# Differential attention with its units in a mixed order, and gates applied as tiles become complete

## The reference

```python
def diff_attn_core(q, k, v, lam):
    s = jnp.einsum('bqhmd,bkhmd->bhmqk', q, k).astype(F32) * (B_HEAD_DIM ** -0.5)
    p = jax.nn.softmax(s, axis=-1)
    a = p[:, :, 0] - lam * p[:, :, 1]
    return jnp.einsum('bhqk,bkhd->bqhd', a.astype(v.dtype), v)

def b_post(o, z, length):
    o = rms_norm(o, subln_w, SUBLN_EPS) * (1.0 - lam_init)
    return o.reshape(bsz, length, B_WIDTH) * jax.nn.silu(z)
```

## Time and profile before

| | |
|---|---|
| median of 3 runs | 1922.96 us (1922.60 to 1924.41) |
| the profiled execution | 1921.78 us, its span 1920.1 us |
| PE busy | 1633.2 us (85%) |
| weight loads of PE | 1167.0 us (61%) |
| DVE busy | 931.6 us (49%) |
| ACT busy | 535.8 us (28%) |
| POOL busy | 150.6 us (8%) |
| DMA | 353.07 MB, mean 184 GB/s |

### The profile page before, as it was taken

One profiled execution on the slowest core, in us unless ns is written; L12 is line 12 of the kernel. 1 busy time (PEld: TensorE's weight loads), 2 busy tenths in 40 slices (PEclk: granted clock), 3 DMA queues, 4 the chain that ended last, 5 costly groups with the idle time before them and its releaser, 6 DMA issues.

```text
span 1920.1 us, 22864 instructions
## 1 busy us (share of the span) xinstructions
PE 1633.2 (85%) x8468; PEld 1167.0 (61%) x8468; DVE 931.6 (49%) x1602; ACT 535.8 (28%) x881; POOL 150.6 (8%) x226
## 2 busy tenths in 40 slices
PE   6799999797969799989499997777699989898980
PEld 6688888586858678777388896466534333333330
DVE  3875634765556556655757674665311111111114
ACT  3313122674132254542422563113111101010111
POOL 1000010132001000000101000110000000000002
PEclk9899999598979899989799997788699999999995
DMA  8224352003223120324134012035399999999993
GB/s 348 88 88 166 114 187 88 12 17 116 99 77 132 66 77 1 131 92 162 65 143 161 1 45 88 1 107 245 128 409 422 422 423 422 423 423 423 422 385 137
DMA packets 55795, 353.07 MB, mean 184 GB/s; under 512 B 7408, under 2 KB 7664, under 8 KB 18720
## 3 DMA queue, kind: packets, MB, share of 16 engines
q1 hardware_dynamic: 43056, 306.88, 39.9%
q0 software_dynamic: 12656, 45.07, 6.3%
HBM read 332.26 MB, written 23.59 MB: 185 GB/s over the span
## 4 chain that ended last, share of the span: by engine, by line
PE 60%; DMA 16%; DVE 15%; ACT 3%; SPq 2%; issue 2%; POOL 1%; DVEq 0%; POOLq 0%; ACTq 0%
PE ps L1834 11%; PE ps L1835 10%; PE ps L1836 10%; DMA early<-in_experts 9%; PE ps L2237 6%; PE ps L2020 5%; PE ps L1884 4%; DMA raw<-in_experts 3%; PE ps L2258 3%; SPq L604 2%; PE ps L2218 2%; PE ps L2042 2%; PE ps L1813 2%; ACT p L847 1%; DMA early<-in_ada 1%
## 5 line engine op out<-in xcount | busy, mean ns | idle before, releaser
L1834 PE MATMUL ps<-whi,xth 128*128 128x512 f32 (+1 forms) x768 | 301.6, 393 | 13.0 <-DVE tmp L1168 4.6
L1835 PE MATMUL ps<-wlo,xth 128*128 128x512 f32 (+1 forms) x768 | 299.1, 389 | 0.0
L1836 PE MATMUL ps<-whi,xtl 128*128 128x512 f32 (+1 forms) x768 | 298.7, 389 | 0.0
L1734 DVE TENSOR_TENSOR hid<-hid,ps 128x256 f32<-128x256 f32 x33 | 13.9, 422 | 370.8 <-ACT hid L1045 370.8
L1834 PEld LDWEIGHTS ps<-whi,xth 128*128 128x128 f32 x768 | 146.4, 191 | 44.8 <-DVE xtl L1161 5.6
L1836 PEld LDWEIGHTS ps<-whi,xtl 128*128 128x128 f32 x768 | 146.5, 191 | 30.0
L1835 PEld LDWEIGHTS ps<-wlo,xth 128*128 128x128 f32 x768 | 146.6, 191 | 28.8
L2237 PE MATMUL ps<-early,xe_t 128*64 128x512 f32 x624 | 142.3, 595 | 14.1 <-DMA early<-in_experts 13.0
L1094 DVE TENSOR_TENSOR wlo<-raw,whi 128x2048 fp32r<-128x2048 f32 (+3 forms) x52 | 103.2, 1985 | 96.4 <-ACT whi L776 81.8
L776 ACT ACTIVATE whi<-raw 128x2048 fp32r<-128x2048 f32 (+2 forms) x46 | 85.5, 1859 | 135.2 <-PE ps L1836 54.6
L2237 PE MATMUL ps<-raw,xe_t 128*64 128x512 f32 x432 | 101.0, 600 | 19.2 <-DMA raw<-in_experts 16.3
(11 more groups left out here) (411 smaller groups left out, 2828.4 us busy)
## 6 DMA issues: line engine op xcount, KB each, us to landing
early<-in_experts SPq DMA_DIRECT2D x129, 1024.0 KB, 26.2
raw<-in_experts SPq DMA_DIRECT2D x54, 1024.0 KB, 26.0
raw<-in_ada SPq DMA_DIRECT2D x40, 1024.0 KB, 6.0
ring<-in_experts SPq DMA_DIRECT2D x15, 1024.0 KB, 27.7
raw<-in_even SPq DMA_DIRECT2D x14, 1024.0 KB, 5.1
raw<-in_second SPq DMA_DIRECT2D x10, 1024.0 KB, 4.9
pair_dram<-tmp POOLq DMA_DIRECT2D x66, 128.0 KB, 5.8
early<-in_ada SPq DMA_DIRECT2D x8, 1024.0 KB, 19.0
```

The costliest lines, as they stand in the source:

```text
L1834: nc.tensor.matmul(v, a[0], b[0], start=first, stop=False)
L1835: nc.tensor.matmul(v, a[0], b[1], start=False, stop=False)
L1836: return nc.tensor.matmul(v, a[1], b[0], start=False, stop=last)
```

## The change

A list `E_ORDER` now gives tile and head of each unit: one context unit, then two latent units, eight times over. The context units go through tiles 0 and 1 head by head, the latent ones through tiles 2 to 5. Written as tile.head the order is 0.0, 2.0, 2.1, 0.1, 2.2, 2.3, 0.2, 3.0, 3.1, 0.3, 3.2, 3.3, 1.0, 4.0, 4.1, 1.1, 4.2, 4.3, 1.2, 5.0, 5.1, 1.3, 5.2, 5.3. PE, ACT and DVE look up the unit's tile and head there. The stagger and the slots stay as they were.

`E_TILES` is the order in which tiles become complete: 2, 0, 3, 4, 1, 5, after unit number 6, 10, 12, 18, 22 and 24. POOL gates the tiles in this order and waits in each case for the sums of squares up to the tile's last unit. The sums stand in their old columns. PE now waits for the low halves of the unit's head before every unit's scores; before it did so for tile 0 only.

```diff
@@ -36,6 +36,10 @@
 R_TABLE = 1152
 S_RUN = {"odd": 16, "gqa": S_UNITS}
 E_UNITS = NT * E_HEADS
+E_ORDER = []
+for _n in range(CT * E_HEADS):
+    E_ORDER += [(_n // E_HEADS, _n % E_HEADS)] + [(CT + _k // E_HEADS, _k % E_HEADS) for _k in (2 * _n, 2 * _n + 1)]
+E_TILES = sorted(range(NT), key=lambda m: E_ORDER.index((m, E_HEADS - 1)))
 KB = 1024
 
 GROUPS, EXPERTS, WIDTH = 4, 32, 512
@@ -648,25 +652,25 @@
                 pool.dma_start(spare[P * i:P * i + P, :], src["x"][i % NT]).then_inc(s_fill, 16)
             pool.dma_start(spare[P * 7:P * 7 + SLOT, :], src["x"][0, 0:SLOT, :]).then_inc(s_fill, 16)
             filled(pool, "mix", "a", 3)
-            for m in range(NT):
-                if m:
-                    pool.wait_ge(s_post, m)
+            for n, m in enumerate(E_TILES):
+                if n:
+                    pool.wait_ge(s_post, n)
                 pool.dma_start(z_in[:], z_dram[m]).then_inc(s_zin, 16)
-                if m == NT - 1:
+                if n == NT - 1:
                     filled(pool, "S", "even", E_UNITS - 1, 1)
-                    for n in range(NT):
-                        pool.dma_start(h_rows[:, n, :], src["x"][n]).then_inc(s_xr, 16)
+                    for a in range(NT):
+                        pool.dma_start(h_rows[:, a, :], src["x"][a]).then_inc(s_xr, 16)
                 z = z_in[:].rearrange("p (h d) -> p h d", d=P)
                 o = o_rows[:, m, :].rearrange("p (h d) -> p h d", d=P)
                 r = orstd[:, 4 * m:4 * m + 4]
-                pool.wait_ge(s_zin, 16 * (m + 1))
+                pool.wait_ge(s_zin, 16 * (n + 1))
                 nc.gpsimd.tensor_tensor(z, z, subln[:].unsqueeze(1).broadcast_to([P, 4, P]), ALU.mult).then_inc(s_zs, 1)
-                pool.wait_ge(s_oss, 4 * (m + 1))
+                pool.wait_ge(s_oss, E_ORDER.index((m, E_HEADS - 1)) + 1)
                 powers(r, oss[:, 4 * m:4 * m + 4], P, SUBLN_EPS, s_ors)
-                pool.wait_ge(s_ors, m + 1)
+                pool.wait_ge(s_ors, n + 1)
                 nc.gpsimd.tensor_tensor(o, o, r.unsqueeze(2).broadcast_to([P, 4, P]), ALU.mult).then_inc(s_orow, 1)
-                pool.wait_ge(s_zs, m + 1)
-                pool.wait_ge(s_orow, m + 1)
+                pool.wait_ge(s_zs, n + 1)
+                pool.wait_ge(s_orow, n + 1)
                 nc.gpsimd.tensor_tensor(o, o, z, ALU.mult).then_inc(s_post, 1)
 
             def row_powers(n, ready):
@@ -836,7 +840,7 @@
                 own(nc.scalar.activation(xth[:, kt, :], v[:, 0:TOK], ACT.Copy), s_xhi)
 
             def exps(u):
-                m = u // 4
+                m = E_ORDER[u][0]
                 for i, pbuf in ((0, p0[:, u % 3, 0:keys(m)]), (1, p1[:, u % 2, 0:keys(m)])):
                     if i == 0 and u >= 3:
                         filled(act, "T", "even", u - 3)
@@ -854,15 +858,16 @@
                 v = filled(act, "T", "even", u)
                 if u >= 2:
                     filled(act, "O", "even", u - 2)
-                n = keys(u // 4)
+                m, h = E_ORDER[u]
+                n = keys(m)
                 own(nc.scalar.activation(pt[:, u % 2, 0:n], v[:, 0:n], ACT.Copy), ev("T", "even", u))
                 if u + 2 < E_UNITS:
                     exps(u + 2)
                 v = filled(act, "O", "even", u)
-                o = o_rows[:, u // 4, P * (u % 4):P * (u % 4) + P]
+                o = o_rows[:, m, P * h:P * h + P]
                 own(nc.scalar.activation(o, v[:, 0:P], ACT.Copy, scale=soft[:, u % 4, 6:7]), ev("O", "even", u))
                 own.free(nc.scalar.activation(junk[:, P * (u % 4):P * (u % 4) + P], o, ACT.Square,
-                                              accum_out=oss[:, u:u + 1]), s_oss)
+                                              accum_out=oss[:, 4 * m + h:4 * m + h + 1]), s_oss)
             for kt in range(4, 8):
                 v = filled(act, "mix", "b", kt)
                 own(nc.scalar.activation(xth[:, kt, :], v[:, 0:TOK], ACT.Copy), s_xhi)
@@ -1258,7 +1263,7 @@
 
             def maxima(u):
                 st = soft[:, u % 4, :]
-                n = keys(u // 4)
+                n = keys(E_ORDER[u][0])
                 for i in range(2):
                     v = filled(dve, "S", "even", u, i)
                     own(nc.vector.tensor_reduce(st[:, 2 + i:3 + i], v[:, 0:n], AX, ALU.max, negate=True), s_nb)
@@ -1935,9 +1940,8 @@
             for m in tiles:
                 evacuated(pe, "even", "bv", m)
             def scores(u):
-                m, h = u // 4, u % 4
-                if m == 0:
-                    pe.wait_ge(s_qk_lo, 2 * h + 2)
+                m, h = E_ORDER[u]
+                pe.wait_ge(s_qk_lo, 2 * h + 2)
                 at_ = slice(P * m, P * m + P)
                 for i in range(2):
                     f = slice(64 * i, 64 * i + 64)
```

## The result

The changed kernel took 1941.27 us (median of 5, 1938.46 to 1949.27) against 1922.96 before: ratio 1.0103, 95% interval [1.0073, 1.0133], some 18 us slower. Forecast was 1931.7 with a range up to 1941.0: right in direction, half the size, just outside the range. Both kernels spread over several microseconds from run to run; the profiled execution of after was the slowest of its five (span 1947.5 us), so I take the second profiled run of the same kernel (again, span 1937.8) for sums.

The account below looks back on a forecast made before the run. The prediction took a DVE-ACT loop to bound the attention stage, with slack on PE. Terms -1.6 + 3.7 + 3.2 + 3.4 = +8.7 us on the median of 1922.96 gave 1931.7 us, range 1926 to 1941.

Parts of the forecast that it names:

- Part 1: Order itself in the DVE-ACT loop: mixed neighbours take 4.26 and 3.46 us, together 7.72 as before; worth 0.
- rival (d): POOL's gate multiplies block DVE's combinations, 1.28 us for each of five tiles: +6.4, 1938 us; chance 0.08.
- Part 2: Latent scores late after context units: one old wait removed, -1.6; six new waits of 0.62 us at full clock, +3.7.
- rival (b): PE's clock stays low longer or falls between units: three further triples at 5.1 us, +15.3 on the forecast, 1947; chance 0.15.
- Part 3: First units at PE's half clock: first place 3.0 us, third unit 0.7 late, 0.5 saved at the start; +3.2 together.
- Part 4: Stage end: POOL's gates late for the last tile, delaying PE's turn of the gated rows by 3.4 us.
- (a): Rival: latent scores not late at all, since PE's queue moves its work forward; +1.3, 1924.3 us; chance 0.13.
- (c): Rival: clock rises at once and stays up through turn (-2.4) and projection (-1.65); +1.5, 1924.5 us; chance 0.06.

Follow-up runs that it names:

- again: Changed kernel once more, unaltered, as base of the follow-up comparisons; ratio 1.0094 to the kernel before.
- warm2: Changed kernel plus nine extra PE products over 128 rows, results unread, around each context unit's scores; ratio 1.0033 to the kernel before.
- tail: Changed kernel with the last tile's gate rows fetched and weighted early and the six residual row loads issued earlier; ratio 1.0104 to the kernel before.
- best: Changed kernel reordered to 4 context, 16 latent, 4 context units, last gates readied early, unread PE products added where PE would wait; ratio 0.9980 to the kernel before.
- best2: Order 4 context, 16 latent, 4 context, gates early, unread products only after the last value product (11) and before the projection (8); ratio 0.9976 to the kernel before.
- oldwarm: Changed kernel put back to the old order, with nine unread PE products around context units' scores, as control; ratio 1.0019 to the kernel before.
- pairs: Changed kernel reordered to two context units, then four latent ones, four times; ratio 1.0005 to the kernel before.
- warm: Changed kernel plus eight PE products over 64 rows, results unread, around each context unit's scores; ratio 1.0079 to the kernel before.

## Why the prediction was wrong

**Part 1** held: context after latent takes 3.40 to 3.45 us from reciprocal to reciprocal (3.46), and latent after context 4.26 where no wait stands before it (once in warm2), as worked out. Seen from the loop alone the order is worth 0, as long as POOL stays out of it (see rival (d)).

**Part 2** had the mechanism and the price at full clock: 0.62 forecast, 0.64 to 0.66 at three places of warm2. The step that failed is "six are left at the full clock". I took it from the old order, where the clock stayed up through all latent units once it had risen, and gave the other case 0.15 as rival (b). In the new order the clock fell at every one of them, which the prediction had named as a sign that it is wrong. The term of the sum, 6 x 0.62 = +3.7, measured +16.3 in again. With 3.8 us I had even priced the wait at half speed nearly rightly (3.57, 3.55, 3.53 measured), but had put only the first place there. Rival (b) is what happened, in all triples instead of three, and each cheaper than its 5.1: the latent unit behind, priced at 1.9, lost nothing (periods of 4.8 us), and at every second place the clock came back before the scores were done, so that a place cost 2.1 to 2.3 us.

**Part 3**: the rise came at 367 us in after and 359 in again, where 364 was forecast. The third unit waited 0.89 (0.7), the first place 2.81 and 0.85 (3.0). The saving of 0.5 at the start is not there: first scores to first reciprocal grew by 0.4.

**Part 4** had the size, 3.4 forecast and 3.2 measured, for the wrong reason. In after and again the low clock of the last two units is what made the end longer, and POOL was ready by the time the last square was; tail shows that freeing POOL gave nothing. The forecast mechanism is real but was covered: with the clock back for the last unit (warm2) POOL was 1.9 us late, and the same edit then gained 1.9.

**Rival (d)** happened, three times in each of three traces: after (396.44, 427.19 and 457.95 us), again (392.65, 423.02 and 453.64) and warm2. In after and again it cost nothing, as PE's scores came later still. POOL's row and then DVE's in again:

```profile
392.65 1.27 POOL L667 TENSOR_TENSOR z_in<-z_in,subln 128x512 f32<-128x512 f32 x1 [2.53 <-DMA z_in<-z_dram]
...
392.65 1.55 DVE L1281 SCALAR_TENSOR_TENSOR p<-p,stat,p 128x256 f32<-128x256 f32 x1
395.30 0.96 DVE L1269 TENSOR_REDUCE stat<-ps 128x1 f32<-128x768 f32 x1 [1.11 <-PE ps L1841]
```

In warm2, where PE was in time, it cost 3.0 us, for three tile ends instead of the five of +6.4. In the trace of before no combination was longer than 1.02 us. The Trainium skill, SBUF — State Buffer, section "Summary: rules for kernel authors", says that of a DVE operation with two SBUF inputs and a GpSimd operation that reads SBUF the second one to issue fully blocks until the first finishes. The rows agree in the main: DVE's combination is 0.9 to 1.1 us longer. Which of the two came first they hardly tell, since both start within 0.16 us of each other, and once (457.95 in after) DVE stands 0.03 us ahead and is longer all the same.

**(a)** and **(c)** did not occur. The prices of (c) for turn and projection were right, though: with the clock held there, in best, they came out at 2.84 us (3.0) and 1.6 saved (1.65). The sum I predicted, +8.7, is close to what the kernel costs with the clock held (+7.3 from first scores to projection in warm2, ratio 1.0033), so the missing 10 us are the clock. That the two agree so well is partly luck: of the 7.3, 3.0 are rival (d), which the sum left out, and the waits of 0.62 show at three places instead of six.

Open is what makes the clock fall. Context units in pairs left it up, single ones didn't; in best2, oldwarm and pairs it fell among latent units where before it hadn't. Warm and warm2 differ in the number of extra products as well as in their rows, so which of the two held it isn't shown either. No experiment here separates this.

## What to carry to other kernels

Before reordering work of unequal size, look at how long PE will be short of work next to each small piece, and price the places behind it at both clock levels; slack that PE has only at 2.4 GHz can be gone when it is needed. When two late things end at the same moment, removing one shows nothing: remove the other first, then try again. An experiment that should hold a state must show in its own trace that it held it, or it says nothing of the theory.

## What the runs showed of the hardware

- Eight extra products over 64 rows per context unit left the clock to fall at four of six places (warm); nine over 128 rows held it at 1.00 for 96 us (warm2). A busy figure near full did not mean that the clock holds: in warm it fell at 436.6 us with PE busy 0.88, 0.65 and 1.00 of the microseconds up to then.
- The clock came back while PE worked without a gap: at 384, 398, 415, 429, 446 and 459 us in after, 3 to 7 us after each fall.
- A combination on DVE beside a multiply of POOL took 1.39 to 1.57 us instead of 0.48 with 256 columns, and 2.06 instead of 1.02 with 768.
- The same kernel spreads by more than I had counted on: the kernel before took 1915.8 to 1931.1 us over all sets, so a single run can be 9 us off the median, and differences below some 3 us had to be read from stretches of a trace.
